# Delta-rule scan: masking the decayed matrix on GpSimd in place of copying its blocks through TensorE

## The reference: what is computed

```python
def _chunked_gated_delta(q, k, v, g, beta, s0):
    ...
    G = jnp.cumsum(g, axis=-1)
    gamma = jnp.exp(jnp.where(incl, G[..., :, None] - G[..., None, :], -jnp.inf))
    kb = k * beta[..., None]
    a_low = jnp.where(strict, jnp.einsum('bhnid,bhnjd->bhnij', kb, k) * gamma, 0.0)
    rhs = jnp.concatenate([v * beta[..., None], kb * jnp.exp(G)[..., None]], axis=-1)
    uw = lax.linalg.triangular_solve(eye + a_low, rhs, left_side=True, lower=True, unit_diagonal=True)
    u, w = uw[..., :dv], uw[..., dv:]
    qk = jnp.einsum('bhnid,bhnjd->bhnij', q, k) * gamma
    ...
    def step(s, inp):
        u_n, w_n, qk_n, qd_n, kd_n, gl_n = inp
        v_new = u_n - jnp.einsum('bhck,bhkv->bhcv', w_n, s)
        o_n = jnp.einsum('bhck,bhkv->bhcv', qd_n, s) + jnp.einsum('bhij,bhjv->bhiv', qk_n, v_new)
        s = s * jnp.exp(gl_n)[..., None, None] + jnp.einsum('bhck,bhcv->bhkv', kd_n, v_new)
        return s, o_n
```

## Time and profile before

| | |
|---|---|
| median of 3 runs | 3621.95 us |
| lowest, highest | 3617.39, 3625.49 us |
| profiled execution, its own time | 3615.66 us |
| its span | 3613.9 us |
| TensorE (PE) busy | 3491.8 us, 97% |
| VectorE (DVE) busy | 2075.0 us, 57% |
| ScalarE (ACT) busy | 861.4 us, 24% |
| GpSimd (POOL) busy | 354.1 us, 10% |
| the two scans | from 1567.7 to about 1773 us, and from 1907.0 to about 2115 us |

### The profile page before, as it was taken

The page is one execution under the profiler, slowest core; times in us unless marked ns, Lnnn a source line. Parts: engine busy times, 40 slices in busy tenths (PEclk is TensorE's granted clock), DMA queues, the critical chain, the costliest instruction groups (busy, mean ns, idle before and its releaser), DMA issues.

```text
span 3613.9 us, 58899 instructions
## 1 busy us (share of the span) xinstructions
PE 3491.8 (97%) x25276; PEld 2875.4 (80%) x25276; DVE 2075.0 (57%) x2875; ACT 861.4 (24%) x1644; POOL 354.1 (10%) x320
## 2 busy tenths in 40 slices
PE   8999999999999999999999999999999899999998
PEld 6777888877778887879897887788888686668886
DVE  3665777647667776655555555522235753864347
ACT  2243001222420013433343321200022103720021
POOL 0000000000100000035204420300000001502000
PEclk9999999999999999999999999999999999999999
DMA  4311544333034444100010031111211331022222
GB/s 169 111 36 56 198 186 163 135 112 98 13 115 186 186 152 156 47 26 3 31 47 15 3 135 59 59 70 59 70 59 70 102 115 47 1 76 99 93 95 92
DMA packets 51459, 320.56 MB, mean 89 GB/s; under 512 B 7132, under 2 KB 7644, under 8 KB 16648
## 3 DMA queue, kind: packets, MB, share of 16 engines
q1 hardware_dynamic: 30240, 220.21, 16.8%
q10 hardware_dynamic: 20968, 96.65, 7.5%
HBM read 299.94 MB, written 9.56 MB: 86 GB/s over the span
## 4 chain that ended last, share of the span: by engine, by line
PE 79%; DVE 7%; PEld 5%; DMA 3%; issue 2%; ACT 2%; PEldq 1%; POOL 0%; ACTq 0%; POOLq 0%; another core or an unknown queue 0%; DVEq 0%; SPq 0%
PE psum L554 20%; PE psum L555 19%; PE psum L556 19%; PE psum L2598 4%; PE psum L2605 4%; DMA pieces_in<-pieces 2%; PEld psum L554 2%; PEld psum L556 2%; PEld psum L555 2%; PE psum L1396 1%; PE psum L1380 1%; PE psum L1369 1%; PE psum L2737 1%; PE psum L750 1%; PE psum L3552 1%
## 5 line engine op out<-in xcount | busy, mean ns | idle before, releaser
L554 PE MATMUL psum<-xt_operands,pieces_hi 128*128 128x512 f32 (+1 forms) x2544 | 938.6, 369 | 20.2 <-DVE xt_operands L810 8.8
L555 PE MATMUL psum<-xt_operands,pieces_hi 128*128 128x512 f32 (+1 forms) x2544 | 927.0, 364 | 0.0
L556 PE MATMUL psum<-xt_operands,pieces_lo 128*128 128x512 f32 (+1 forms) x2544 | 926.7, 364 | 0.0
L554 PEld LDWEIGHTS psum<-xt_operands,pieces_hi 128*128 128x128 f32 x2544 | 480.5, 189 | 106.8 <-issue 15.3
L554 PE MATMUL psum<-pieces_hi,xt_operands 128*128 128x512 f32 x1338 | 531.3, 397 | 13.4 <-DVE pieces_lo L601 9.4
L556 PEld LDWEIGHTS psum<-xt_operands,pieces_lo 128*128 128x128 f32 x2544 | 480.1, 189 | 77.0
L555 PEld LDWEIGHTS psum<-xt_operands,pieces_hi 128*128 128x128 f32 x2544 | 480.8, 189 | 73.0
L555 PE MATMUL psum<-pieces_lo,xt_operands 128*128 128x512 f32 x1338 | 523.4, 391 | 0.0
L556 PE MATMUL psum<-pieces_hi,xt_operands 128*128 128x512 f32 x1338 | 523.4, 391 | 0.0
L611 DVE TENSOR_TENSOR pieces_lo<-pieces_in,pieces_hi 128x2048 fp32r<-128x2048 f32 x190 | 443.6, 2335 | 5.3
L568 DVE CAST pieces_hi<-pieces_in 128x2048 fp32r<-128x2048 f32 x190 | 237.6, 1251 | 303.0 <-PE psum L554 147.1
(11 more groups left out here) (383 smaller groups left out, 4146.5 us busy)
## 6 DMA issues: line engine op xcount, KB each, us to landing
pieces_in<-pieces SPq DMA_DIRECT2D x210, 1024.0 KB, 4.9
x_mem<-ada ACTq DMA_DIRECT2D x28, 1024.0 KB, 4.9
arena<-ada ACTq DMA_DIRECT2D x20, 1024.0 KB, 4.8
arena<-mods ACTq DMA_DIRECT2D x8, 512.0 KB, 16.0
arena<-arena ACTq DMA_DIRECT2D x32, 128.0 KB, 4.3
xt_values<-arena ACTq DMA_DIRECT2D x8, 384.0 KB, 9.2
x_park<-x_mem ACTq DMA_DIRECT2D x1, 3072.0 KB, 13.8
o_park<-arena ACTq DMA_DIRECT2D x2, 1536.0 KB, 5.4
```

The costliest lines, as they stand in the source:

```text
L554: signal_later(k, pe.matmul(out, sh, mh, start=start, stop=False))
L555: signal_later(k, pe.matmul(out, sh, ml, start=False, stop=False))
L556: return pe.matmul(out, sl, mh, start=False, stop=stop)
```

## The change

The two plain copies of ul go: ul is then 16 instructions of 64x64 in half a bank. ulm masks the transposed blocks alone (128x256). A new operation `lm` on GpSimd multiplies low by a mask that has `b16` in its two diagonal blocks of 64 and zero elsewhere (128x512, into buffer t, both operands in SBUF); a1 reads its plain blocks from there, so it waits for lm as well as ulm, and diff of the next step waits for a1, which now reads t. `lvm` takes the blocks from low itself: two operations of 64 partitions by 256 columns with both operands in SBUF, in place of one from PSUM. The mask is written in the projection stage of each half by a memset and two copies on VectorE. In the order of TensorE ul.0 comes one product sooner (before su.1' and kk.1, with kk.1 behind su.1'); on VectorE lvm.0 moves from before low.1 to behind ulm.1; on GpSimd lm.0 stands behind dlow.1 and lm.1 behind x1.0. A bank of ul counts as emptied with ulm.

```diff
--- before.py
+++ after.py
@@ -1911,6 +1911,7 @@
     k.modcol = k.mod_all.rearrange("p (l w a b) -> p l w a b", l=DEPTH, w=6, b=2)
     rt_at = lasting.at
     k.rt = lasting.take(2, 512)
+    k.diagonal16 = k.rt[:, 1, P:2 * P]
     rows = Arena(k.arena_operands, rt_at, rt_at + 1024)
     k.prefix_rows, k.pick = rows.take(512), rows.take(512)[:, 0:2 * NT2]
     k.c2 = lasting.take(N_C2)
@@ -2211,6 +2212,13 @@
     dve.tensor_copy(hi, k.ps[ROW_PARTS[0], 4, :])
     e.link(dve.tensor_copy(lo, k.ps[ROW_PARTS[1], 4, :]))
     e.link(dve.tensor_tensor(lo, k.ps[ROW_PARTS[1], 4, :], lo.bitcast(F32), ALU.subtract))
+
+
+def diagonal_mask_dve(k, dve, e):
+
+    e.link(dve.memset(k.diagonal16, 0.0))
+    for r in (slice(0, 64), slice(64, P)):
+        dve.tensor_copy(k.diagonal16[r, r], cols(C2, k.c2, "b16")[r, :])
 
 
 def qkv_pe(k, e, slot, _):
@@ -2402,6 +2410,7 @@
         dve.memset(k.conv[i][:, 512:516], 0.0).then_inc(S.padding_ready, 1)
     taps = cols(DN, k.dn, "conv", 12, 5)
     split_dve(k, e, 1)
+    diagonal_mask_dve(k, dve, e)
     prefix_pick_dve(k, dve, e)
     for n in range(N_QKV):
         if n % 2 == 0 and 2 <= n < N_QKV - 2:
@@ -2449,12 +2458,13 @@
 ORDERS = {
     "pe": order("a3.0' x4.0' a1.1' x8.0' ks.1' wy.0' x2.1' a2.1' qk.1' xx0.0' a3.1' z0.0' x4.1' y1.0' o1.1' x8.1' "
       "xx1.0' gb.0 wy.1' w2.0' y2.0' gb.1 xx0.1' xx2.0' z0.1' y1.1' vn.0' xx1.1' o1.0' w2.1' y2.1' o2.0' "
-      "xx2.1' su.0' vn.1' kk.0 o2.1' qk.0 kk.1 ul.0 su.1' a1.0 ks.0 a2.0 x2.0 ul.1 "),
-    "dve": order("diff.0 wya.1' diff.1 v2a.0' v2a.1' t1.0' t2.0' s2.0' low0.0 low.0 qg.0 ulm.0 t2.1' low0.1 lvm.0 "
-      "low.1 s2.1' r1.0 x2a.0 ulm.1 x4a.0 rr.0 x8a.0 lvm.1 wya.0 r1.1 rr.1 x2a.1 qg.1 x4a.1 x8a.1 t1.1 "),
+      "xx2.1' su.0' vn.1' kk.0 o2.1' qk.0 ul.0 su.1' kk.1 a1.0 ks.0 a2.0 x2.0 ul.1 "),
+    "dve": order("diff.0 wya.1' diff.1 v2a.0' v2a.1' t1.0' t2.0' s2.0' low0.0 low.0 qg.0 ulm.0 t2.1' low0.1 "
+      "low.1 s2.1' r1.0 x2a.0 ulm.1 lvm.0 x4a.0 rr.0 x8a.0 lvm.1 wya.0 r1.1 rr.1 x2a.1 qg.1 x4a.1 x8a.1 t1.1 "),
     "act": order("y1c.0' v1c.0' w2c.0' y2c.0' xf.1' z0c.1' y1c.1' v1c.1' vnc.0' w2c.1' y2c.1' gamt.0 vnc.1' gam.0 "
       "gam.1 l2c.0 l4c.0 l8c.0 gamt.1 l2c.1 l4c.1 xf.0 l8c.1 z0c.0 "),
-    "pool": order("x1.1' kd.0' s1.1' s1.0' dup.0 dlow.0 oa.0' dup.1 dlow.1 x1.0 kd.1 bv.1 bv.0 oa.1' "),
+    "pool": order("x1.1' kd.0' s1.1' s1.0' dup.0 dlow.0 oa.0' dup.1 dlow.1 lm.0 x1.0 lm.1 kd.1 bv.1 "
+      "bv.0 oa.1' "),
 }
 
 
@@ -2473,7 +2483,7 @@
 
 AT = counted(N_STEPS)
 PE_AT = {n: key for key, (engine, n) in AT.items() if engine == "pe"}
-TAKEN = dict(gb="diff", kk="low0", qk="qg", ul="lvm", a1="l2c", x2="x2a", a2="l4c", x4="x4a", a3="l8c", x8="x8a", wy="wya", xx0="xf", z0="z0c", y1="y1c", xx1="v1c", w2="w2c", y2="y2c", xx2="v2a", ks="r1", vn="vnc", o1="t1", o2="t2", su="s2")
+TAKEN = dict(gb="diff", kk="low0", qk="qg", ul="ulm", a1="l2c", x2="x2a", a2="l4c", x4="x4a", a3="l8c", x8="x8a", wy="wya", xx0="xf", z0="z0c", y1="y1c", xx1="v1c", w2="w2c", y2="y2c", xx2="v2a", ks="r1", vn="vnc", o1="t1", o2="t2", su="s2")
 IN_BLOCKS = ("xx0",)
 RINGS = ((1, 7), (0, 1))
 
@@ -2641,13 +2651,8 @@
         if not runs(s):
             return
         ready(s, d, "ul", ("low",))
-        low, out = low_of(k, s, d), middle2(k, "ul", s, d)
-        for h in range(HALF):
-            for r in PAIRED:
-                pe.matmul(out[r, 0, h, :], low[r, h, r], eye[r, :], start=True, stop=True)
-        for r in PAIRED:
-            last = pe.matmul(out[r, 1, :, :], eye[r, :], low[r, :, r], start=True, stop=True)
-        st.done(last)
+        low = low_of(k, s, d)
+        st.done(blocks(middle(k, "ul", s, d), lambda h, r: low[r, h, r], lambda h, r: eye[r, :], PAIRED))
 
     def square(s, d, name, src, *needs):
 
@@ -2659,7 +2664,12 @@
         st.done(blocks(out[:, 0, :, :], of(d, src, 1), of(d, src, 0), PAIRED))
 
     def a1(s, d):
-        square(s, d, "a1", "l1", "ulm")
+        if not runs(s):
+            return
+        ready(s, d, "a1", ("ulm", "lm"))
+        out, lower, upper = middle2(k, "a1", s, d), lambda h, r: k.buf[d]["t"][r, h, r], of(d, "l1", 0)
+        blocks(out[:, 1, :, :], upper, lower, PAIRED)
+        st.done(blocks(out[:, 0, :, :], lower, upper, PAIRED))
 
     def a2(s, d):
         square(s, d, "a2", "l2", "l2c")
@@ -2770,7 +2780,7 @@
         o1(t - 1, 1); x8(t - 1, 1); xx1(t - 1, 0); gb(t, 0); wy(t - 1, 1); w2(t - 1, 0); y2(t - 1, 0); gb(t, 1)
         xx0(t - 1, 1); xx2(t - 1, 0); z0(t - 1, 1); y1(t - 1, 1); vn(t - 1, 0); xx1(t - 1, 1); o1(t - 1, 0)
         w2(t - 1, 1); y2(t - 1, 1); o2(t - 1, 0); xx2(t - 1, 1); su(t - 1, 0); vn(t - 1, 1); kk(t, 0)
-        o2(t - 1, 1); qk(t, 0); kk(t, 1); ul(t, 0); su(t - 1, 1); a1(t, 0); ks(t, 0); a2(t, 0); x2(t, 0)
+        o2(t - 1, 1); qk(t, 0); ul(t, 0); su(t - 1, 1); kk(t, 1); a1(t, 0); ks(t, 0); a2(t, 0); x2(t, 0)
         ul(t, 1)
 
 
@@ -2890,7 +2900,7 @@
         return step_column(k, i, s, d) if runs(s) else None
 
     def diff(s, d):
-        tt(s, d, "diff", k.buf[d]["t"], ps("gb", s, d), col(PRE, s, d), ALU.subtract, "gb")
+        tt(s, d, "diff", k.buf[d]["t"], ps("gb", s, d), col(PRE, s, d), ALU.subtract, "gb", "-a1")
 
     def low0(s, d):
         t = k.buf[d]["t"]
@@ -2905,14 +2915,17 @@
 
     def ulm(s, d):
         if runs(s):
-            mask = cols(C2, k.c2, "b16").unsqueeze(1).broadcast_to([P, 2 * HALF, 64])
-            tt(s, d, "ulm", k.buf[d]["l1"].rearrange("p a h c -> p (a h) c"),
-               middle2(k, "ul", s, d).rearrange("p a h c -> p (a h) c"), mask, ALU.mult, "ul")
+            mask = cols(C2, k.c2, "b16").unsqueeze(1).broadcast_to([P, HALF, 64])
+            tt(s, d, "ulm", k.buf[d]["l1"][:, 0, :, :], middle(k, "ul", s, d), mask, ALU.mult, "ul")
 
     def lvm(s, d):
-        if runs(s):
-            mask = cols(C2, k.c2, "corner16").unsqueeze(1).broadcast_to([P, HALF, 64])
-            tt(s, d, "lvm", k.buf[d]["lv"], middle2(k, "ul", s, d)[:, 1, :, :], mask, ALU.mult, "ulm")
+        if not runs(s):
+            return
+        st.begin("lvm", s, d, ("low",))
+        for r in PAIRED:
+            last = dve.tensor_tensor(k.buf[d]["lv"][r, :, :], low_of(k, s, d)[r, :, r],
+                                     cols(C2, k.c2, "corner16")[r, :].unsqueeze(1).broadcast_to([64, HALF, 64]), ALU.mult)
+        st.done(last)
 
     def grow(s, d, name, src, *needs):
         if runs(s):
@@ -2958,8 +2971,8 @@
 
     for t in range(N_STEPS + 1):
         diff(t, 0); wya(t - 1, 1); diff(t, 1); v2a(t - 1, 0); v2a(t - 1, 1); t1(t - 1, 0); t2(t - 1, 0)
-        s2(t - 1, 0); low0(t, 0); low(t, 0); qg(t, 0); ulm(t, 0); t2(t - 1, 1); low0(t, 1); lvm(t, 0); low(t, 1)
-        s2(t - 1, 1); r1(t, 0); x2a(t, 0); ulm(t, 1); x4a(t, 0); rr(t, 0); x8a(t, 0); lvm(t, 1); wya(t, 0)
+        s2(t - 1, 0); low0(t, 0); low(t, 0); qg(t, 0); ulm(t, 0); t2(t - 1, 1); low0(t, 1); low(t, 1)
+        s2(t - 1, 1); r1(t, 0); x2a(t, 0); ulm(t, 1); lvm(t, 0); x4a(t, 0); rr(t, 0); x8a(t, 0); lvm(t, 1); wya(t, 0)
         r1(t, 1); rr(t, 1); x2a(t, 1); qg(t, 1); x4a(t, 1); x8a(t, 1); t1(t, 1)
 
 
@@ -2993,6 +3006,9 @@
         tt(s, d, "x1", k.buf[d]["xc"], k.buf[d]["l1"][:, 0, :, :], cols(C2, k.c2, "eye").unsqueeze(1).broadcast_to([P, HALF, 64]),
            ALU.add, "ulm")
 
+    def lm(s, d):
+        tt(s, d, "lm", k.buf[d]["t"], low_of(k, s, d), heads(k.diagonal16), ALU.mult, "low")
+
     def bv(s, d):
         tt(s, d, "bv", k.buf[d]["rr"], chunk(k.vc_, s, d), col(BETA, s, d), ALU.mult)
 
@@ -3010,7 +3026,7 @@
 
     for t in range(N_STEPS + 1):
         x1(t - 1, 1); kd(t - 1, 0); s1(t - 1, 1); s1(t - 1, 0); dup(t, 0); dlow(t, 0); oa(t - 1, 0); dup(t, 1)
-        dlow(t, 1); x1(t, 0); kd(t, 1); bv(t, 1); bv(t, 0); oa(t - 1, 1)
+        dlow(t, 1); lm(t, 0); x1(t, 0); lm(t, 1); kd(t, 1); bv(t, 1); bv(t, 0); oa(t - 1, 1)
```

## The result

The changed kernel takes 3635.63 us, median of 6 runs (3632.74 to 3640.64), against 3621.76 (3617.39 to 3625.49, 6 runs) for the kernel before: a ratio of 1.0039, 95% interval 1.0026 to 1.0052. It is slower, by 9 to 19 us. The profiled execution of after took 3635.67 us with a span of 3633.8, beside 3615.66 and 3613.9 of before.

What follows compares the result with a forecast made beforehand. TensorE, busy all turn, was taken as the bound, replaced by a chain through GpSimd. Ten turns by 1.79 us gave +17.9 on 3615.66; the same step on the median 3621.95 gave 3639.9 us, range 3618 to 3648.

Steps and rivals of the forecast that it cites:

- Ten turns by 1.79: Scan: each of ten turns (five a half, working on steps 1 to 5) grows by 1.79 us, +17.9 us in all.
- the fill: First turn of each half: 0.44 saved at ul.1, about as much lost at lvm.0; 0, within 0.5 either way.
- a1.0 late on lm.0: TensorE's a1.0 waits for GpSimd's lm.0 behind dlow.1: 1.1 us of new idle time, 0.67 later than before.
- The forecast's 1614.2: Time in the profiled turn at which TensorE would be ready for a1.0, against 1614.66 before.
- x8.0 late on the split lvm: lvm.0's halves wait for bv.0 and oa.1 on GpSimd; x8.0 starts at 1622.91, idle 1.5 us; turn grows 1.79.
- the price of a wait: A wait between two engines, such as TensorE's copies to VectorE's ulm.0, costs 0.05 us.
- (1): Rival: lvm.0's halves run without GpSimd between, or lvm.0 asks before bv.0 starts; +7 us, 3629; chance 0.22.
- (2): Rival: half-height operations don't meet the lock, or come when GpSimd idles; +1 to +2 us, 3623; chance 0.15.
- (3): Rival: lm.0 isn't late for a1.0, so 0.9 us a turn is gained; -10 us, 3612; chance 0.10.
- (4): Rival: more waits join (x1.1, rr.0 holding x8a.0) or the clock drops; +28 us, 3650; chance 0.09.
- kk.1's new place: TensorE: kk.1 later costs nothing, since its reader low0.1 waits for an exponential anyway; otherwise under 0.9 us.
- ul.1's 0.44: TensorE: removing direction 1's two copies in ul.1 gives 0.44 us a turn back.

Runs made afterwards that it cites:

- Run 5: Changed kernel with lm.0 ahead of dup.1 on GpSimd and nothing else: 3636.80 us in one run (kernel before 3626.25).
- run 2: Changed kernel with lvm as one 128x256 SBUF operation instead of two halves (output not the program's): 3618.15 us in one run (kernel before 3621.67).
- run 3: Changed kernel with x1.1 ahead of oa.1' in GpSimd's order: 3632.62 us in one run.
- run 7: Changed kernel with TensorE's copies and full ulm back and lm gone, keeping the split SBUF lvm at its new place: 3631.29 us in one run.
- version 8: Changed kernel with lm.0 first, lvm.0 early, bv.0 and x1.1 ahead of oa.1', bv.1, kd.1: 3606.52 us, ratio 0.9949 to kernel before; again 3607.86, 0.9965.
- run 6: Changed kernel with kk.1 back ahead of ul.0 on TensorE: 3639.99 us in one run.
- run 4: Changed kernel with lvm.0 early on VectorE, between t2.1' and low0.1: 3619.75 us in one run.
- run 9: As version 8, but with lm.0 between dup.1 and dlow.1 on GpSimd: 3604.66 us, ratio 0.9960 to the kernel before (3617.97).

## Why the prediction was right

**The sign and the size.** 3639.9 was forecast, with 3618 to 3648, and 3635.6 measured. Ten turns by 1.79 made +17.9 us; the scans of the profiled execution grew by 19.5, and its own time by 20.0. The median of the runs grew by 13.9, as the profiled execution of before was 6.1 us under its median and that of after stood on its own. That the forecast of the median is off by no more than 4.3 us is in part luck: the turn was put 2.9 us too low over ten turns, the fill 1.6 too high, and the difference of 6 us between profile and median, which the forecast carried over, wasn't there in after.

**a1.0 late on lm.0.** Forecast 4.52 after o2.1's end and 1.1 us of idle time; measured 4.60 and 1.04. lm took 1.27, forecast 1.26. Run 5 confirms the cause: with lm.0 first, a1.0 comes at TensorE's own 3.50. The forecast's 1614.2 makes 3.4; the rest is ul.0, 0.62 us to the next product (1648.94 to 1649.56) and not 0.51.

**x8.0 late on the split lvm.** Forecast 7.58 after a1.0; measured 7.73. Counted from lm.0's end (E=1652.51), bv.0 was to end at E+5.57 (it did, 1658.09), lvm.0 to ask at E+4.73 (E+4.78), oa.1' to get in at E+5.70 (E+5.71), the second half to end at E+7.23 (E+7.27). The Trainium skill, SBUF — State Buffer, Terms and Who interferes with whom, has the first starter keep the shared port pair for the full instruction; the rows agree for operations with two SBUF inputs, save for the last 0.13 to 0.15 us of an instruction, in which the next owner is already in, if it then takes its undisturbed length (1657.95 against 1658.09, 1658.22 against 1658.37, 1659.36 against 1659.49). Runs 2 and 3 show that the lock is handed over between instructions: the same work as one instruction costs 1.08 us, as two 2.49.

**What was mis-sized.** The turn missed 34.58 by 0.29. x8.0 came 0.23 too late after o2.1: the second half 0.04, x4a.0 behind it 0.10 (0.45 from the half's end to its own, where I had 0.35), and the price of a wait 0.09. That price I had taken (0.05 to 0.06) from the copies and ulm.0, where VectorE waits for TensorE. A TensorE that has stood idle starts 0.14 to 0.15 behind the end of what releases it (lm.0 1652.51, a1.0 1652.65; x4a.0 1660.23, x8.0 1660.38), and so in run 7. At a1.0 this costs the turn nothing, as x8.0's chain counts from lm.0 through GpSimd's queue. The last 0.06 is the stretch from x8.0 to o2.1.

**The fill.** Forecast 0; in these two profiles it was a gain of about 1.6 us, which brings ten turns of 2.08 down to the 19.5 measured (with 0.3 of scatter). The first a1.0 comes 0.29 later after the scan's start in each half, but the way from a1.0 to x8.0 becomes shorter. The windows of before are 16 us near the start of the first half in four pieces, then a1.0 to x8.0 of the first turn of either half, then of a later turn:

```profile
1571.00:1575.00 4.00, 0.09 (x1) 0.00 (x0) 1.11 (x3) 1.26 (x2) 3.84 (x4) 1.00 0.01 2
1575.00:1579.00 4.00, 1.97 (x20) 1.15 (x20) 2.52 (x4) 0.63 (x1) 0.76 (x1) 0.50 0.00 0
1579.00:1583.00 4.00, 3.87 (x40) 3.56 (x40) 2.43 (x4) 0.60 (x1) 3.85 (x4) 0.50 0.00 0
1583.00:1587.00 4.00, 4.00 (x91) 3.81 (x92) 1.54 (x3) 0.60 (x1) 0.33 (x1) 0.72 0.02 4
...
1579.13:1588.30 9.17, 9.17 (x172) 8.67 (x174) 4.90 (x8) 2.10 (x4) 5.13 (x6) 0.67 0.01 2
1918.43:1926.98 8.55, 8.55 (x173) 8.04 (x175) 4.91 (x8) 2.10 (x4) 5.13 (x6) 0.72 0.01 2
1614.66:1621.12 6.46, 6.46 (x174) 6.12 (x174) 5.19 (x10) 2.15 (x5) 6.15 (x7) 1.00 0.01 3
```

and of after, a1.0 to x8.0 in the same order:

```profile
1582.48:1590.17 7.69, 6.97 (x169) 6.62 (x169) 5.00 (x9) 2.69 (x5) 6.02 (x6) 0.87 0.01 2
1931.63:1939.33 7.70, 6.56 (x170) 6.26 (x169) 5.42 (x9) 2.70 (x5) 6.02 (x6) 0.94 0.02 3
1652.65:1660.38 7.73, 6.19 (x169) 5.89 (x169) 6.16 (x10) 2.69 (x5) 7.10 (x8) 1.00 0.01 2
```

After TensorE has stood nearly idle (0.09 us of 4) its granted clock is 0.50, which is 1.2 GHz, and the first turn of before runs from a1.0 to x8.0 partly at it, at a mean of 0.67 and 0.72: TensorE is busy throughout and takes 9.17 and 8.55 in place of 6.46. In after x8.0 waits for VectorE, so that a part of the slow products falls into what would be idle time, and the mean is higher besides (0.87, 0.94). That it comes to 7.7 us as in later turns is chance: bv.0 ends 5.9 us after a1.0 in place of 5.4, and x1.1 (0.73 us) gets in between the halves where later turns have oa.1' (1.27). I priced the fill in operations of VectorE and left out the 0.89 of the earlier trace rows, which I had shown.

How much of the 1.6 us belongs to the change isn't shown, since the clock of this stretch differs between executions and halves. The same stretch in the two profiles of version 8, and then in the second half of run 6:

```profile
1582.46:1589.91 7.45, 7.45 (x170) 7.21 (x170) 4.80 (x8) 2.73 (x5) 5.16 (x6) 0.78 0.01 2
1588.15:1594.12 5.97, 5.97 (x169) 5.78 (x170) 4.71 (x8) 2.61 (x5) 4.65 (x5) 0.99 0.01 3
1933.73:1943.10 9.37, 8.95 (x168) 8.50 (x169) 4.57 (x9) 2.46 (x5) 6.71 (x7) 0.66 0.01 2
```

One and the same kernel takes 1.5 us more in it at a mean clock of 0.78 than at 0.99, and run 6, whose x8.0 is as late as after's in later turns, takes 9.37 at 0.66.

**The rivals.** (1), no GpSimd between the halves, and (2), no meeting with GpSimd: both fall by rows (oa.1' starts between the halves; 1078 against 422 ns), and by runs 2 and 3. (1)'s edge was 0.25 us away (bv.0 starts at 1657.04, lvm.0 asks at 1657.29). (3), lm.0 not late, falls by the 1.04 us. (4) didn't come: x1.1 ends 2.4 us before x2.1 starts, wy.0 isn't late. It does come in runs 4 and 5, once x8.0 is earlier.

**Costs of nothing.** kk.1's new place (run 6) and the ulm of half the width held; both, and diff's new wait, are in runs 8 and 9 as well, whose turns are shorter than before's. That ul.1's 0.44 comes back is borne out by run 4: x8.0 after a1.0 6.46 before, 5.99 with lvm.0 out of the way.

## What to carry to other kernels

Before an operand moves from PSUM to SBUF, look at what GpSimd runs at that time: here a VectorE operation with two SBUF inputs queued behind GpSimd's current instruction (0.41 us became 1.08), and split in two it let GpSimd in again between the parts (2.49). A new helper operation belongs ahead of the point where the critical chain passes that engine's queue, and a VectorE operation exposed to such queueing belongs where VectorE waits anyway; the same change, so ordered, turned 14 us of loss into 13 of gain (run 9; each against the kernel before, measured beside it). Expect the next wait behind the one that was removed (runs 4, 5 and 8), and trace the whole turn for it.

## What the runs showed that was not expected

- An operation of 64 partitions by 256 columns takes 0.40 to 0.42 us, as one of 128 by 256 does: half the partitions save nothing, and the split costs an instruction even without GpSimd.
- Whole executions of one kernel scatter by more than the changes inside them: 3613.9 to 3635.1 us for the kernel before over all runs of it, and 3617.0 to 3635.1 on one chip alone. Within an execution single turns are longer by 0.2 to 1.6 us than their neighbours with the same instructions, in every version (the second half of before has turns of 32.80, 32.96, 33.16 and 33.08). What causes that stays open; versions with one run are therefore judged here by their turns, and not by their times.
- Not tried: lvm at its new place with a PSUM operand and without the copies, since low isn't in PSUM there.
